# Two neighbouring weight slots taken together, with 512 moving columns, where results have tokens on the partitions

## The reference, cut to what matters

```python
# block 1: w_in is 1024 x 2496; hi_ are its columns 1024 to 1535
u = rms_norm(h, ln_mix[i]) @ w_in[i]
hq, hf, hi_, hg, cq, ckv, kr = jnp.split(u, split_at, axis=-1)
# hi_ holds the values of hgrn2_chunkwise (4 heads x 128)

# block 2: w_in is 1024 x 5648; after the pool columns come q, k, v, 1024 each
z = jnp.einsum('bsd,de->bse', h, w_in[l])
v = z[..., o:o + ATTN_W].reshape(B, S, ATTN_HEADS, HEAD_DIM)
```

## Time and profile before

| | before |
|---|---|
| median of 3 runs | 1757.26 us |
| lowest, highest | 1751.45, 1759.26 us |
| span of the profiled execution | 1757.0 us |
| TensorE busy | 1352.4 us (77%) |
| VectorE busy | 1005.0 us (57%) |
| ScalarE busy | 563.4 us (32%) |
| GpSimd busy | 973.5 us (55%) |
| mean granted TensorE clock | 0.885 |

### The profile page before, as it was taken

How to read it: one execution, slowest core, us unless ns; L and a number is a source line. 1 busy time by engine, 2 the same in 40 slices (tenths; PEclk the granted TensorE clock), 3 DMA queues, 4 the chain that set the end, 5 groups by cost and what they waited for, 6 DMA issues and landing times. The chain is left out here.

```text
span 1757.0 us, 22117 instructions
## 1 busy us (share of the span) xinstructions
PE 1352.4 (77%) x7568; PEld 1041.1 (59%) x7568; DVE 1005.0 (57%) x1747; ACT 563.4 (32%) x887; POOL 973.5 (55%) x698
## 2 busy tenths in 40 slices
PE   5999989868998986988878676656664676666658
PEld 4999989758998985977768532222221232222223
DVE  5886444465886346226346886666645666566341
ACT  4443344235443445444344321112111211312111
POOL 2444356213443443875645777677676777777763
PEclk9999999889999998999989987778887888888779
DMA  8676434105774531442234799999998999999995
GB/s 321 248 274 228 161 140 148 57 24 186 272 267 185 180 132 41 153 144 89 102 120 176 240 366 345 346 346 357 357 349 307 377 358 350 353 359 355 346 348 215
DMA packets 96068, 427.07 MB, mean 243 GB/s; under 512 B 10672, under 2 KB 10992, under 8 KB 77424
## 3 DMA queue, kind: packets, MB, share of 16 engines
q0 software_dynamic: 73728, 268.47, 41.4%
q1 hardware_dynamic: 20736, 149.96, 23.7%
q10 hardware_dynamic: 1520, 7.60, 1.1%
HBM read 424.93 MB, written 1.05 MB: 242 GB/s over the span
## 5 line engine op out<-in xcount | busy, mean ns | idle before, releaser
L288 POOL TENSOR_TENSOR wlo<-ring,whi 128x1024 fp32r<-128x1024 f32 x162 | 405.8, 2514 | 531.2 <-ACT whi L856 530.6
L778 PE MATMUL ps<-v_rows,diag 128*128 128x512 f32 x512 | 285.5, 641 | 266.8 <-DMA v_rows<-in_expert_v,arena 250.4
L1547 DVE CUSTOM_DVE_ANT_0 arena<-arena 128x1024 f32<-128x1024 f32 x256 | 324.2, 1266 | 182.8 <-DMA arena<-in_expert_u,arena 141.6
L382 PE MATMUL ps<-nh,whi 128*128 128x256 f32 x1440 | 369.9, 293 | 35.1 <-ACT nh L870 27.3
L383 PE MATMUL ps<-nh,wlo 128*128 128x256 f32 x1440 | 362.9, 288 | 0.0
L856 ACT ACTIVATE whi<-ring 128x1024 fp32r<-128x1024 f32 x236 | 245.1, 1055 | 363.2 <-PE ps L387 177.5
L778 PEld LDWEIGHTS ps<-v_rows,diag 128*128 128x128 f32 x512 | 103.0, 205 | 402.6 <-DMA v_rows<-in_expert_v,arena 262.3
L1666 POOL DMA_INDIRECT arena<-in_expert_u,arena x256 | 282.3, 1103 | 98.3 <-issue 81.2
L1666 POOL DMA_INDIRECT v_rows<-in_expert_v,arena x256 | 260.6, 1018 | 132.7 <-issue 85.0
L382 PEld LDWEIGHTS ps<-nh,whi 128*128 128x128 f32 x1440 | 283.8, 197 | 40.9 <-issue 26.0
L383 PEld LDWEIGHTS ps<-nh,wlo 128*128 128x128 f32 x1440 | 284.4, 198 | 0.4
(11 more groups left out here) (255 smaller groups left out, 1372.7 us busy)
## 6 DMA issues: line engine op xcount, KB each, us to landing
ring<-in_w SPq DMA_DIRECT2D x118, 1024.0 KB
arena<-in_wmod SPq DMA_DIRECT2D x24, 1024.0 KB, 4.8
arena<-in_expert_u,arena POOLq DMA_INDIRECT x256
v_rows<-in_expert_v,arena POOLq DMA_INDIRECT x256
small<-in_small ACTq DMA_DIRECT2D x1, 2816.0 KB, 19.3
h<-in_x ACTq DMA_DIRECT2D x1, 1024.0 KB, 7.9
keys<-in_keys ACTq DMA_DIRECT2D x1, 1024.0 KB, 25.3
out<-arena SPq DMA_DIRECT2D x2, 512.0 KB, 3.9
```

The lines of the kernel that those rows point to most:

```text
L288: return v.tensor_tensor(wlo[:, tile % TILES, :], ring[:, tile // 2 % RAW, at:at + TILE], whi[:, tile % TILES, :].bitcast(F32), ALU.subtract)
L382: mm(to, hi[:, k, :], nh[:, k, :], start=(k == 0), stop=False)
L778: mm(ps[:, acc, :], diag[:, k, :], vbuf[:, g % RV, 0:512], start=False, stop=False, skip_group_check=True)
L1547: own(v.tensor_tensor_reduce(out=e["junk"], in0=ubuf[:, g % RU, :], in1=h2[:, b, :], scale=1.0, scalar=0.0, op0=ALU.mult, op1=ALU.add, acc ...
```

## The change

`tokens(n)` now takes slots n and n + 1, that is all four tiles of `whi` and `wlo`. It waits for the four tiles, and for each half of the tokens runs 8 x 3 matmuls of 512 moving columns, one half into bank `n % 4`, the other into the next. It counts four tiles at its end. It is called once in the first stage (the second call, after `level(2)`, is gone), and twice in the second. ScalarE's copies out of PSUM keep their number and size and their places in its order; each now takes one bank. On the host two blocks of 256 columns of the first weight are exchanged, since there the pair's first slot lies in the second half of the ring.

```diff
             def tokens(n):
-                r = bank(n)
-                tile = 2 * weight_slot(n)
-                split_tile(tile)
-                split_tile(tile + 1)
-                at = tile % TILES
-                hi, lo = (w[:, at:at + 2, :].rearrange("p t (k n) -> p t k n", k=C) for w in (whi, wlo))
+                first = 2 * weight_slot(n)
+                for tile in range(first, first + TILES):
+                    split_tile(tile)
+                hi, lo = (w[:, :, :].rearrange("p t (k n) -> p t k n", k=C) for w in (whi, wlo))
                 for b in range(TB):
+                    to = ps[:, bank(n + b), :].rearrange("p (t n) -> p t n", t=TILES)
+                    cols = slice(b * P, (b + 1) * P)
                     for k in range(C):
-                        cols = slice(b * P, (b + 1) * P)
-                        to = pair(r)[:, b, :]
                         mm(to, nh[:, k, cols], hi[:, :, k, :], start=(k == 0), stop=False)
                         mm(to, nh[:, k, cols], lo[:, :, k, :], start=False, stop=False)
                         last = mm(to, nl[:, k, cols], hi[:, :, k, :], start=False, stop=(k == C - 1))
-                last.then_inc(S("tiles_done"), 2)
+                last.then_inc(S("tiles_done"), TILES)
...
             tokens(S_IN + 6)
             latent_sums()
             level(2, hqf, hk)
-            tokens(S_IN + 7)
             for n in (1, 2, 3, 4):
                 q_up(n)
...
-            for base, step in ((S_IN2, features), (S_IN2 + 4, features), (S_IN2 + 8, tokens)):
-                for j in range(4):
...
+            for j in range(8):
+                features(S_IN2 + j, split_at=None if j else 5)
+            for j in range(8, 12, 2):
+                tokens(S_IN2 + j)
...
-                copied(S_IN + 6 + j, fn(hv[:, :, j * T:(j + 1) * T], pair((S_IN + 6 + j) % BANKS), ACT.Copy))
+                copied(S_IN + 6 + j, fn(hv[:, j, :], ps[:, (S_IN + 6 + j) % BANKS, :], ACT.Copy))
...
-                copied(S_IN2 + 8 + j, fn(v2[:, :, j * T:(j + 1) * T], pair((S_IN2 + 8 + j) % BANKS), ACT.Copy))
+                at = slice(j // TB * 2 * T, (j // TB + 1) * 2 * T)
+                copied(S_IN2 + 8 + j, fn(v2[:, j % TB, at], ps[:, (S_IN2 + 8 + j) % BANKS, :], ACT.Copy))
```

More of the change, by code:

```diff
@@ L1766 @@
         gate_up(x["w1_gate"], x["w1_up"]), blocks(x["w1_down"][0]),
-        blocks(np.concatenate([w_in[:, 512:1024], w_in[:, 0:512], latent, w_in[:, 1024:2048]], 1)),
+        blocks(np.concatenate([w_in[:, 512:1024], w_in[:, 0:512], latent, w_in[:, 1280:1536],
+                               w_in[:, 1024:1280], w_in[:, 1536:2048]], 1)),
         blocks(x["w_out"][0]),
```

## The result

The changed kernel took 1789.08 us (median of 4 runs, 1787.18 to 1795.08) against 1755.63 us (4 runs) for the kernel before, timed beside it: ratio 1.0188, 95% interval 1.016 to 1.0215. It is 33 us slower; 34 were forecast. The profiled execution's span is 1793.3 us and its time 1795.08, so 1.8 us lie outside the span.

The account below looks back on a forecast made before the run. TensorE was taken to bound `tokens`, with the fill hidden beneath it. First stage 7.3 + 1.5, second 17.4 + 0.5 and clock 7.2 sum to 33.9 us on 1757.0: 1791 us, own range 1784 to 1797, wider range 1778 to 1800.

Parts of the forecast that it names:

- The pair is as long as two slots: Both stages' tokens matmuls: 0.23 us per 512-column matmul, 11.0 us a pair against 11.5; three pairs save 1.5 us.
- The rival of a far cheaper matmul: Tokens pairs: weight loads bound the stream, so a pair takes 6.3 us; total 1777 us; chance 0.06.
- First pair starts late: First stage: the pair needs the fourth tile, so it starts at 285.4 us instead of 283.28.
- The chain ahead of `q_up`: First stage: 9.7 us from pair's end to `q_up` lies bare, making it 7.3 us late; slower scalings add 1.5.
- Pair 1 and pair 2: Second stage's two tokens pairs: TensorE idles 7.2 and 11.0 us ahead of them; scores come 17.4 us late.
- The clock: TensorE restarts at 1.2 GHz after new idle ahead of `q_up`, pair 1 and pair 2: three at 2.4, 7.2 us.
- The 1.9 us of idle ahead of the first pair: First stage: this short idle was costed at nothing in clock, up to 2.2 us.
- The softmax behind the scores: After the second stage: GpSimd's subtractions run into the first softmax's start, costing 0.5 us (0 to 1.2).
- the rival on the other side: Expert fetches from 947.85 us on have slack that absorbs the delay; not slower, 1756 us; chance 0.04.
- The rival of a clock that stays low through a pair: Second stage's pairs run at 0.43 us a matmul, 20.6 us each, adding 14.4 us; total 1805; chance 0.09.

Follow-up runs that it names:

- the kernel with all three edits: Changed kernel with latent_sums ahead of the first pair, six second-stage slots' subtractions on VectorE, and the count in two parts; ratio 1.0085 to the kernel before.

## Why the prediction was right, point by point

- **The pair is as long as two slots.** 0.23 us a matmul were taken; 48 took 11.01 us at full clock, 0.229 each (starts at 288.79, 289.02 and 289.25 in the changed kernel). The rival of a far cheaper matmul, 0.13 us each, falls: halving the number of matmuls and weight loads took 11.58 us only to 11.01.
- **First pair starts late.** From `level(1)` to the pair 1.7 us before and 4.0 after, so 2.3; 2.1 forecast.
- **The chain ahead of `q_up`.** 9.7 + 1.5 = 11.2 us were forecast from the pair's end, 11.7 measured. All of the excess over 9.7 is the two scalings, 2.92 us instead of 0.88. That the chain alone held `q_up` is shown by putting it earlier, which took all but 0.2 us of this stage's loss away.
- **Pair 1 and pair 2.** Idle 7.2 and 11.0 forecast, 6.97 and 10.73 measured; 5.3 ahead of the scores, 5.06 measured. Splitting the count in two moved the last two as computed. A faster subtraction moved pair 1 and pair 2 as well, by 3.3 and 4.4 us, where 1.9 and 3.5 were computed. Pair 1's number is right by a step that was partly wrong: slot 9's landing and two subtractions were forecast, slot 8's landing and four subtractions in a row set it (746.69 + 1.14 + 9.31 + 0.25 = 757.39). The two ways end within 0.6 us of each other, counted from the short wait in the features.
- **The clock.** Three restarts at 2.4 were forecast. The pairs took 13.62 and 13.38, so 2.6 and 2.4 over 11.01; `q_up` 8.69, only 1.4 over 7.25. In the other profiles with an idle stretch ahead of `q_up` its restart cost 1.4 to 2.8. Filling the stretches removed all three.
- **What was wrong.** The 1.9 us of idle ahead of the first pair was costed at nothing in clock. In this profile it was 2.09, the clock fell, and the pair took 12.53 us, 1.5 more. That more than made up for `q_up`'s cheaper restart (1.0 us less). The softmax behind the scores was given 0.5 us; from the scores to TensorE's next work (L490 before, L488 after) it is 18.9 before and 19.1 after, so 0.2. Even this is gone a few us later, where the clock stood at 1.00 after and at 0.50 before (L694 before and L689 after come 23.3 and 22.1 us behind the scores).
- **Sum.** Forecast 33.9, of which 0.5 lie behind the scores; measured 12.5 + 21.4 = 33.9 up to the scores and 0.2 behind them. That it agrees to some tenths is luck: the first stage came out 1.3 us over its 11.2 (7.3 + 1.5 + 2.4), the second 0.8 under its 22.2 (17.4 + 4.8), and single terms were off by 1.5 us on one side and 1.0 on the other. The first fetch of experts moved from 947.85 to 980.75, 32.9 later, with the same 4.24 us of wait for VectorE's indices:

```profile
980.75 1.11 POOL L1662 DMA_INDIRECT arena<-in_expert_u,arena  x1 [4.24 <-DVE arena L1533]
```

The scores came 34.1 us later, so what lies between takes 1.2 us back and no more (the clock behind the first scores), and the rival on the other side falls. The rival of a clock that stays low through a pair falls too: it costs 2.4 to 2.6 us a pair, where that rival has 9.6.

Open stays why the part behind the scores varies between 976 and 993 us from profile to profile. Open is also when the clock falls after 2 to 4 us of idle; what the profiles show of it is told below.

## What to carry to other kernels

Before an instruction stream is regrouped, ask how many buffer places one group holds: if it holds all of them, the filling engines and the matrix engine take turns, and the fill goes onto the path, here 7 us ahead of one group and 11 us ahead of the next. Work that stood between two groups may have been the cover of another chain; find what waits behind it, since putting that chain ahead was worth 12 of 34 us here. Price a saving per instruction at full clock from a stream (0.57 us a pair here) and set it against a restart of the clock (1.4 to 2.8 us here), which any new idle stretch of a few us can bring.

## What the runs showed of the hardware

- After about 2.0 us of idle time the clock sometimes fell and sometimes didn't. Ahead of the first pair it was idle for 2.00 to 2.09 us in seven profiles: the pair behind it began at the lower level in three (2.09, 2.00, 2.00) and ran at the upper in four (2.01, 2.00, 2.00, 2.00). With the clock fallen, the window 284.80 to 288.00 of the changed kernel reads:

```profile
284.80:288.00 3.20, 3.12 (x8) 0.50 0.71 238
```

- Longer stretches do not settle it either. After 2.85 us of idle in the kernel before (784.96) the granted clock was 0.50, after 3.04 us in the changed one (819.23) it was 1.00. In the kernel with all three edits it fell only when TensorE was at work again: pair 2 started at 756.73 after 3.80 us of idle, the clock was 0.92 from 756.70 to 758.20 and 0.50 from 758.20 to 760.70. So a first matmul of normal length does not show that no restart follows.
- A subtraction of two tensors on GpSimd holds up VectorE's instructions that read two tensors from the shared memory (0.88 us for two became 2.92 to 3.08, 0.69 for one became 2.74 to 2.83), but not its reciprocal of one (3.35 either way).
- VectorE does the same subtraction of 128x1024 in 1.18 us when GpSimd is quiet, half of GpSimd's 2.33.
